# A split-product decoder trunk: all low-part subtractions on VectorE, the norm's squares on ScalarE

## The chip, the cores and the metric

The kernel runs on one core of one Trainium2 chip. The metric is the device time of one execution in microseconds; the median of three runs of the kernel before is 1012.09 us (1011.86 to 1013.77). Names: PE is TensorE (matmul), PEld its weight load, DVE is VectorE, ACT is ScalarE, POOL is GpSimd, SP is the engine that issues the loads of weights.

## What is computed

Two layers of a decoder trunk over N = 288 token columns: a prompt of 256 and 8 groups of 4 sampled tokens. The model width is 1024, kept as X[128, 8, 288]: 8 tiles of 128 features.

```python
for l in range(DEPTH):                       # 2 layers
    h  = rmsnorm(x, g_mix) @ w_in            # mixer: attention, a gated recurrence, a short convolution
    x  = x + concat(a, o_h, o_c) @ w_out
    x  = x + cross_attn(rmsnorm(x, g_xattn)) @ w_xo
    u  = rmsnorm(x, g_ffn) @ w_up            # 1024 -> 2 * 2816
    a, b = split(causal_dwconv3(u))
    x  = x + (silu(a) * b) @ w_down          # 2816 -> 1024
y = rmsnorm(x, g_final)
```

Inputs and outputs are fp32.

## The kernel before

Products of the mixer's input and output projections and of the FFN are "split": an operand v is written as hi + lo, where hi is v rounded to the type fp32r (by ScalarE, a cast) and lo = v - hi (a subtraction, its result fp32r too). A product is then three matmuls of 128x128 weights with 128x288 columns: hi hi, hi lo, lo hi (`split_product`, L1219, L1220, L1221). Both operands need it: the weights, the normalised input (scaled by the gain only; the 1/rms is applied to the product's result), the mixer's results and the FFN's hidden tiles.

One list of steps (`layer_schedule`) sets the order of the work on every engine. Each engine walks the list and does its own part of each step; semaphores tie them. TensorE fills 8 banks of PSUM in turn.

The up stage has 22 tiles per layer (i = 0 to 21). Tile i has two halves (ab = 0, 1), each 8 split products, so 48 matmuls for a tile. In one turn of the loop come, in this order:

- `round` of the weights of tile i + 2 (ScalarE cast of 128x2048, L1116),
- half 0 on TensorE; VectorE evicts it from PSUM times 1/rms (L1885, L1886); GpSimd copies two small pieces of it (L909, L910); ScalarE multiplies by the first tap (L1157),
- `convolve` of tile i - 1: four fused multiply-adds on VectorE (L1894), then a silu on ScalarE (L1162),
- half 1 likewise,
- `pads` of tile i + 1 on GpSimd (two memsets L901, two small copies L902),
- `gate` of tile i - 1: VectorE forms the hidden tile hT (L1903, L1904), ScalarE casts it (L1166), GpSimd subtracts to get hT_lo (L886),
- `rest` of tile i + 2: the weights' lo. VectorE does the first 1024 columns (L1630), GpSimd the other 1024 (L875). TensorE waits for both before tile i + 2.

For w_down a chunk holds 8, 8 or 6 tiles of 256 columns; VectorE does 3 tiles (768 columns) and GpSimd the rest. For w_in and w_out VectorE does all 1024 columns.

```python
LO_DVE = {"in": 8, "out": 8, "up": 4, "down": 3}         # tiles of the weights' lo on VectorE
# GpSimd, step "rest", L870:
pool.wait_ge(w_hi, count)
cols = slice(LO_DVE[args[0]] * width, tiles * width)
pool.drain()
g_.tensor_tensor(lo[:, cols], both[:, cols], hi_part[:, cols].bitcast(F32), ALU.subtract).then_inc(w_lo_pool, 1)
```

The residual adds: after each result tile m of `out`, `xo` and `down` VectorE adds it to X[:, m] (L1555), squares the sum (L1545, L1547) and adds the square to `acc` (L1549). A ones matmul (`ssq`) sums `acc` over the features, and 1/rms is made by ScalarE and four VectorE instructions. ScalarE scales X[:, m] by the next norm's gain into fp32 `XG` (L963) and, after `xo` and `down`, rounded into the hi part (L965, L967); GpSimd subtracts the two to get `xg_lo` (L881, L919), for which TensorE waits in each first split product. At the very end (`down` of the last layer) the same chain leads to the final norm.

Of the kernel before, what the change touches and what calls it, by code (L numbers as in the profile page):

```python
# [28 lines left out]
ALU = mybir.AluOpType  # L29
# [6 lines left out]
P = 128  # L36
# [45 lines left out]
LO_DVE = {"in": 8, "out": 8, "up": 4, "down": 3}  # L82
# [333 lines left out]
def decoder_kernel(nc, a, out):  # L416
# [4 lines left out]
    with ExitStack() as ctx:  # L421
# [39 lines left out]
        def ph(*shape, parts=P):  # L461
# [80 lines left out]
        xg_lo = rounded["XG"]  # L542
        ring_lo = rounded["ring"]
# [33 lines left out]
            "x_square", "sumsq", "xg_tile", "mg_even", "mg_odd", "rms_guess", "sigmoids", "gates_ready", "silu_gate_in",  # L577
# [6 lines left out]
        w_lo_dve = sem("w_lo_dve")  # L584
        w_lo_pool = sem("w_lo_pool")
# [18 lines left out]
        def split_of(kind, i, l):  # L604


            if kind in ("in", "out"):
# [7 lines left out]
                    ring_hi[split % SLOTS], 256, tiles)  # L615

# [115 lines left out]
        def _(pool):  # L732
# [34 lines left out]
            for l, step, args, who in banks.steps:  # L767
# [102 lines left out]
                elif step == "rest" and args[0] in ("up", "down"):  # L870
                    count, both, lo, hi_part, width, tiles = split_of(*args)
                    pool.wait_ge(w_hi, count)
                    cols = slice(LO_DVE[args[0]] * width, tiles * width)
                    pool.drain()
                    g_.tensor_tensor(lo[:, cols], both[:, cols], hi_part[:, cols].bitcast(F32),  # L875
                                     ALU.subtract).then_inc(w_lo_pool, 1)
                elif step == "xo":
                    k = args[0]
                    pool.wait_ge(s["xg_hi"], KT_D * (2 * l + 1) + k + 1)
                    pool.drain()  # L880
                    g_.tensor_tensor(xg_lo[:, k], XG[:, k], xg_hi[k].bitcast(F32), ALU.subtract).then_inc(s["xg_lo"], 1)  # L881
                elif step == "gate":
                    i = args[0]
                    pool.wait_ge(s["h_hi"], FT * l + i + 1)
                    pool.drain()
                    g_.tensor_tensor(hT_lo[:, i], hT[:, i], hT_hi[:, i].bitcast(F32), ALU.subtract).then_inc(s["h_lo"], 1)  # L886
# [25 lines left out]
                elif step == "down" and l + 1 < DEPTH:  # L912
                    k = args[0]
                    if k == 0:
                        pe_done(pool, l, "up", FT - 1, 1)
                        layer_loads(l + 1)
                    pool.wait_ge(s["xg_hi"], KT_D * (2 * l + 2) + k + 1)
                    pool.drain()
                    g_.tensor_tensor(xg_lo[:, k], XG[:, k], xg_hi_mix[:, k].bitcast(F32), ALU.subtract).then_inc(s["xg_lo"], 1)  # L919
# [10 lines left out]
        def _(act):  # L930
# [21 lines left out]
            def gained(l, stage, k):  # L952
# [9 lines left out]
                if stage or l:  # L962
                    ac(XG[:, k], X[:, k], ACT.Identity, scale=par[:, c:c + 1]).then_inc(s["xg_tile"], 1)  # L963
                if stage == 0:
                    ac(xg_hi_mix[:, k], X[:, k], ACT.Identity, scale=par[:, c:c + 1]).then_inc(s["xg_hi"], 1)  # L965
                if stage == 2:
                    ac(xg_hi[k], X[:, k], ACT.Identity, scale=par[:, c:c + 1]).then_inc(s["xg_hi"], 1)  # L967

            for l, step, args, who in banks.emptying_steps:
# [115 lines left out]
                elif (step, args) == ("out", (7,)):  # L1085
                    pe_done(act, l, "hstate_s", 1)
                    for k in range(KT_D):
                        gained(l, 1, k)
# [95 lines left out]
        def _(pe):  # L1184
# [23 lines left out]
            def xg(l, stage, k):  # L1208
                pe.wait_ge(s["xg_tile"], 24 * l + 8 * stage + k + 1 - KT_D)
                return XG[:, k]  # L1210

            def project(out_, w, cols, l, stage):
                for k in range(KT_D):
                    last = mm(out_[:, 0:N], w[:, k, cols], xg(l, stage, k), start=k == 0, stop=k == KT_D - 1)  # L1214
                return last
# [14 lines left out]
            for l, step, args, who in banks.steps:  # L1230
# [209 lines left out]
                elif step == "xq":  # L1440
                    last = project(o, whole(l, P_XQ + args[0]), slice(0, P), l, 1)
# [76 lines left out]
                elif step == "y":  # L1518
# [3 lines left out]
                    pe.wait_ge(s["xg_tile"], 24 * DEPTH - KT_D + 4 * h + 4)  # L1522
# [8 lines left out]
        def _(dve):  # L1531
# [9 lines left out]
            def squares(k, stage):  # L1541

                drain()
                if k == 0:
                    v.tensor_tensor(acc[:], X[:, k], X[:, k], ALU.mult)  # L1545
                else:
                    v.tensor_tensor(sqr[:], X[:, k], X[:, k], ALU.mult)  # L1547
                    drain()
                    last = v.tensor_tensor(acc[:], acc[:], sqr[:], ALU.add)  # L1549
                    if k == KT_D - 1:  # L1550
                        last.then_inc(s["sumsq"], 1)
# [33 lines left out]
            for l, step, args, who in banks.emptying_steps:  # L1585
# [40 lines left out]
                elif step == "rest":  # L1626
                    count, both, lo, hi_part, width, tiles = split_of(*args)
                    dve.wait_ge(w_hi, count)
                    cols = slice(0, LO_DVE[args[0]] * width)
                    v.tensor_tensor(lo[:, cols], both[:, cols], hi_part[:, cols].bitcast(F32),  # L1630
                                    ALU.subtract).then_inc(w_lo_dve, 1)
# [267 lines left out]
                elif step == "gate":  # L1899
# [5 lines left out]
                                    ALU.mult).then_inc(s["h_tile"], 1)  # L1905

# [26 lines left out]
```

## Time and profile before

| what | value |
|---|---|
| median of 3 runs | 1012.09 us (1011.86 to 1013.77) |
| span of the profiled execution | 1012.0 us, 0.1 us under the median |
| PE, PEld | 932.8 us (92%), 869.0 us (86%) busy |
| DVE | 680.2 us (67%) |
| ACT | 435.5 us (43%) |
| POOL | 460.2 us (45%) |

Matmuls are pipelined: the busy time of one (about 0.29 us) overlaps that of the next, which starts 0.13 us after it. So TensorE is best read by the starts of its matmuls and by the idle time before them. The profile gives no time of the profiled execution apart from its span.

### The profile page before, as it was taken

Reading aid. Unit: us, or ns where it says so; the run is one execution under the profiler, and the core shown is the slowest. Engines: PE = TensorE matmul, PEld = TensorE weight load, DVE = VectorE, ACT = ScalarE, POOL = GpSimd, SP = SyncE. Lnnn points to the kernel's source line nnn. Section 1 sums busy time; section 2 is a strip of 40 time slices with the busy share of each in tenths; the row PEclk is TensorE's granted clock in tenths of the full one; section 3 lists DMA queues with packets and bytes.
Section 4 is the critical chain, followed back from the end, with each engine's and each line's share of the span. In section 5 each row is a group of like instructions: output and inputs, shape, how many; then the busy total and the mean of one; then the engine's idle time right before and its main releaser. Section 6 shows DMA issues by size and latency. Waiting matters only on the chain.

```text
span 1012.0 us, 17881 instructions
## 1 busy us (share of the span) xinstructions
PE 932.8 (92%) x6566; PEld 869.0 (86%) x6566; DVE 680.2 (67%) x1260; ACT 435.5 (43%) x728; POOL 460.2 (45%) x701
## 2 busy tenths in 40 slices
PE   6889999998988889889989999999898899898996
PEld 4889988986788888889989998898588888888996
DVE  5567863654459999984455886276345999999533
ACT  4543541434545454444444254143355454453432
POOL 1412310422347777767651231043134777777651
PEclk9989997998689999999999999889868999999999
DMA  8745521566145454445557552139704454453442
GB/s 250 192 114 149 161 72 34 143 183 199 34 118 141 127 159 131 139 143 167 158 147 181 166 166 82 42 98 229 199 1 125 126 163 129 135 158 115 157 146 64
DMA packets 209409, 137.71 MB, mean 136 GB/s; under 512 B 23475, under 2 KB 202203, under 8 KB 209323
## 3 DMA queue, kind: packets, MB, share of 16 engines
q1 hardware_dynamic: 199904, 111.11, 39.2%
q0 software_dynamic: 8288, 22.85, 7.8%
q10 hardware_dynamic: 1131, 2.62, 0.7%
q8 instruction: 53, 0.87, 0.4%
q14 instruction: 33, 0.27, 0.1%
HBM read 131.11 MB, written 5.44 MB: 135 GB/s over the span
## 4 chain that ended last, share of the span: by engine, by line
PE 59%; POOL 16%; ACT 9%; issue 8%; DVE 4%; DMA 1%; POOLq 1%; DVEq 1%; ACTq 0%; SPq 0%
PE banks L1219 12%; PE banks L1220 11%; PE banks L1221 11%; POOL ring_r L875 10%; ACT keysT_r L1116 3%; ACT vals_r L1116 3%; POOL phase L909 3%; PE banks L1397 3%; PE banks L1479 2%; PE banks L1362 2%; PE banks L1319 2%; PE banks L1214 2%; POOL phase L902 1%; PE banks L1447 1%; PE banks L1313 1%
## 5 line engine op out<-in xcount | busy, mean ns | idle before, releaser
L1221 PE MATMUL banks<-mix_r,ring_r 128*128 128x288 f32 x1008 | 302.1, 300 | 0.0
L1894 DVE SCALAR_TENSOR_TENSOR phase<-phase,fpar 128x304 f32<-128x304 f32 x176 | 196.6, 1157 | 4.0 <-issue 0.4
L1221 PEld LDWEIGHTS banks<-mix_r,ring_r 128*128 128x128 f32 x1008 | 195.3, 194 | 0.0
L1219 PE MATMUL banks<-mix_r,ring_r 128*128 128x288 f32 x480 | 151.6, 316 | 9.0 <-issue 6.6
L875 POOL TENSOR_TENSOR ring_r<-ring,keysT_r 128x1024 fp32r<-128x1024 f32 (+2 forms) x36 | 98.9, 2746 | 52.2 <-ACT keysT_r L1116 48.4
L1220 PE MATMUL banks<-XG_r,keysT_r 128*128 128x288 f32 x384 | 115.3, 300 | 0.0
L1219 PEld LDWEIGHTS banks<-mix_r,ring_r 128*128 128x128 f32 x480 | 94.3, 196 | 15.4 <-issue 12.0
L1220 PE MATMUL banks<-XG_r,ring_r 128*128 128x288 f32 x352 | 107.0, 304 | 0.0
L1219 PE MATMUL banks<-mix_r,keysT_r 128*128 128x288 f32 x288 | 89.2, 310 | 18.3 <-POOL ring_r L875 17.0
L1116 ACT CAST ring_r<-ring 128x1024 fp32r<-128x1024 f32 x60 | 62.5, 1046 | 97.9 <-DMA ring<-in_w_in 71.6
L1221 PE MATMUL banks<-phase_r,ring_r 128*128 128x288 f32 x352 | 103.1, 293 | 0.0
L1220 PE MATMUL banks<-XG_r,vals_r 128*128 128x288 f32 x320 | 94.4, 295 | 0.0
L875 POOL TENSOR_TENSOR ring_r<-ring,vals_r 128x1024 fp32r<-128x1024 f32 (+2 forms) x32 | 84.5, 2641 | 12.5 <-ACT vals_r L1116 8.0
L1219 PE MATMUL banks<-mix_r,vals_r 128*128 128x288 f32 x240 | 72.2, 301 | 15.8 <-POOL ring_r L875 15.8
L1630 DVE TENSOR_TENSOR ring_r<-ring,ring_r 128x1024 fp32r<-128x1024 f32 x60 | 74.7, 1247 | 14.5 <-ACT ring_r L1116 14.1
L1162 ACT ACTIVATE phase<-phase 128x304 f32<-128x304 f32 x44 | 20.2, 460 | 136.0 <-DVE phase L1894 136.0
L1116 ACT CAST keysT_r<-ring 128x2048 fp32r<-128x2048 f32 (+1 forms) x36 | 66.8, 1861 | 22.1 <-DMA ring<-in_w_down 22.1
L1219 PEld LDWEIGHTS banks<-mix_r,keysT_r 128*128 128x128 f32 x288 | 55.5, 193 | 23.1 <-issue 21.1
L1630 DVE TENSOR_TENSOR ring_r<-ring,keysT_r 128x1024 fp32r<-128x1024 f32 (+1 forms) x36 | 43.7, 1213 | 47.0 <-ACT keysT_r L1116 47.0
L1220 PEld LDWEIGHTS banks<-XG_r,keysT_r 128*128 128x128 f32 x384 | 74.1, 193 | 0.2
L1220 PEld LDWEIGHTS banks<-XG_r,ring_r 128*128 128x128 f32 x352 | 69.3, 197 | 0.2
L909 POOL COPY phase<-phase 128x2 f32<-128x2 f32 x88 | 31.3, 356 | 83.1 <-DVE phase L1886 82.9
(298 smaller groups left out, 2311.7 us busy)
## 6 DMA issues: line engine op xcount, KB each, us to landing
ring<-in_w_up SPq DMA_DIRECT2D x88, 512.0 KB, 5.1
ring<-in_w_in SPq DMA_DIRECT2D x36, 512.0 KB, 3.9
ring<-in_w_down SPq DMA_DIRECT2D x16, 1024.0 KB, 5.2
ring<-in_w_down SPq DMA_DIRECT2D x8, 768.0 KB, 4.9
rawk<-in_cache_k POOLq DMA_DIRECT2D x32, 128.0 KB, 2.6
vals<-in_cache_v POOLq DMA_DIRECT2D x32, 128.0 KB, 2.4
ring<-in_w_in SPq DMA_DIRECT2D x16, 256.0 KB, 4.0
rawk<-in_cache_mem_k POOLq DMA_DIRECT2D x16, 256.0 KB, 4.7
```

What stands on the lines that cost most here:

```text
L875: g_.tensor_tensor(lo[:, cols], both[:, cols], hi_part[:, cols].bitcast(F32), ALU.subtract).then_inc(w_lo_pool, 1)
L909: g_.tensor_copy(ulast[:, j, g, 0:2], u[:, 256:258])
L1116: nc.scalar.copy(hi_part[:, 0:tiles * width], both[:, 0:tiles * width]).then_inc(w_hi, 1)
L1214: last = mm(out_[:, 0:N], w[:, k, cols], xg(l, stage, k), start=k == 0, stop=k == KT_D - 1)
L1219: mm(out_, hi_w, hi_x, start=start, stop=False)
L1220: mm(out_, hi_w, lo_x, start=False, stop=False)
L1221: return mm(out_, lo_w, hi_x, start=False, stop=stop)
L1319: last = mm(o[:, P * c:P * c + P], mg[:, k, P * t:P * t + P], w[:, k], start=k == 0, stop=k == KT_D - 1)
L1362: last = mm(o[:, 0:256], qs[:, P * b:P * b + P], keysT[:, p, b], start=b == 0, stop=b == 7)
L1397: last = mm(o[0:n, at:at + n // 2], hk[r, p, c], q, start=True, stop=True)
L1630: v.tensor_tensor(lo[:, cols], both[:, cols], hi_part[:, cols].bitcast(F32), ALU.subtract).then_inc(w_lo_dve, 1)
L1894: last = v.scalar_tensor_tensor(out=y[ab][:, 0:304], in0=uab[i % 2][ab][:, w:304 + w], scalar=fpar[:, 3 * l + w, c:c + 1], in1=y[ab][:, 0: ...
```

## The change

All subtractions that make a lo part go to VectorE, and the squares of the residual sum to ScalarE:

- `rest` of w_up and w_down: VectorE subtracts all columns (2048, or 1536 in a short chunk) in one instruction; GpSimd has none. One semaphore, `w_lo`, takes the place of two.
- hT_lo: VectorE subtracts tile i - 1 behind the gate of tile i (the last two behind the last gate).
- xg_lo: VectorE makes X * gain - hi in one fused instruction, one tile behind its residual add, as the prologue of the kernel does already (L1593). ScalarE no longer writes the fp32 `XG` where nothing else reads it (after `xo`, and after `down` except in the last layer).
- ScalarE squares X[:, k] into two buffers in turn; VectorE adds them to the sum, one tile behind its residual add. In `out` the last square stands behind the eight scalings of the next norm.
- GpSimd keeps its small copies, memsets and DMAs.

```diff
-LO_DVE = {"in": 8, "out": 8, "up": 4, "down": 3}
@@ GpSimd
-                elif step == "rest" and args[0] in ("up", "down"):
-                    ...
-                elif step == "xo":
-                    ...
-                elif step == "gate":
-                    i = args[0]
-                    pool.wait_ge(s["h_hi"], FT * l + i + 1)
-                    pool.drain()
-                    g_.tensor_tensor(hT_lo[:, i], hT[:, i], hT_hi[:, i].bitcast(F32), ALU.subtract).then_inc(s["h_lo"], 1)
-                elif step == "down" and l + 1 < DEPTH:
+                elif (step, args) == ("down", (0,)) and l + 1 < DEPTH:
+                    pe_done(pool, l, "up", FT - 1, 1)
+                    layer_loads(l + 1)
@@ ScalarE
-                if stage or l:
+                if stage in (1, 3):
                     ac(XG[:, k], X[:, k], ACT.Identity, scale=par[:, c:c + 1]).then_inc(s["xg_tile"], 1)
...
+            def square(l, step, k):
+                wait_emptied(act, l, step, k)
+                if k >= 2:
+                    act.wait_ge(s["sq_added"], (KT_D - 2) * (3 * l + squared[step] - 1) + max(1, k - 2))
+                ac(sq[k % 2][:], X[:, k], ACT.Square).then_inc(s["x_square"], 1)
...
+                elif step == "out":
+                    if args[0]:
+                        square(l, step, args[0] - 1)
+                    if args[0] == 7:
+                        pe_done(act, l, "hstate_s", 1)
+                        for k in range(KT_D):
+                            gained(l, 1, k)
+                        square(l, step, 7)
                 elif step == "xo":
                     ...
                     gained(l, 2, args[0])
+                    square(l, step, args[0])
                 elif step == "down":
                     ...
+                    square(l, step, args[0])
@@ TensorE
-                pe.wait_ge(w_lo_dve, count)
-                if kind in ("up", "down"):
-                    pe.wait_ge(w_lo_pool, count - SPLIT_PIECES * (l + 1))
+                pe.wait_ge(w_lo, count)
@@ VectorE
+            def summed(l, step, k):
+                if k:
+                    dve.wait_ge(s["x_square"], squares_before(l, step) + k + 1)
+                    drain()
+                    last = v.tensor_tensor(acc[:], sq[0][:] if k == 1 else acc[:], sq[k % 2][:], ALU.add)
+                    last.then_inc(s["sq_added"] if k < KT_D - 1 else s["sumsq"], 1)
+
+            def xg_rest(l, step, k):
+                ...
+                v.scalar_tensor_tensor(out=xg_lo[:, k], in0=X[:, k], scalar=par[:, c:c + 1], in1=hi_part.bitcast(F32),
+                                       op0=ALU.mult, op1=ALU.subtract).then_inc(s["xg_lo"], 1)
...
                 v.tensor_tensor(X[:, m], X[:, m], b_[:, 0:N], ALU.add).then_inc(emptied["D"], 1)
-                squares(m, 0)
+                for k in {0: (), KT_D - 1: (m - 1, m)}.get(m, (m - 1,)):
+                    if step == "xo" or (step == "down" and l + 1 < DEPTH):
+                        xg_rest(l, step, k)
+                    summed(l, step, k)
...
-                    cols = slice(0, LO_DVE[args[0]] * width)
+                    cols = slice(0, tiles * width)
                     v.tensor_tensor(lo[:, cols], both[:, cols], hi_part[:, cols].bitcast(F32),
-                                    ALU.subtract).then_inc(w_lo_dve, 1)
+                                    ALU.subtract).then_inc(w_lo, 1)
...
+                    for t in {0: (), FT - 1: (i - 1, i)}.get(i, (i - 1,)):
+                        dve.wait_ge(s["h_hi"], FT * l + t + 1)
+                        v.tensor_tensor(hT_lo[:, t], hT[:, t], hT_hi[:, t].bitcast(F32), ALU.subtract).then_inc(s["h_lo"], 1)
```

## Rows read from the trace of the kernel before

**Rows 1.** Busy time by stage: us, busy (instructions) of each engine, clock, DMA share, GB/s
```profile
301.20:443.60 142.40, 125.94 (x912) 122.00 (x912) 135.56 (x210) 68.44 (x95) 105.47 (x191) 1.00 0.50 139
```

**Rows 2.** TensorE's timeline: start, us, matmul, [idle before it <- releaser]
```profile
301.21 0.37 PE L1219 MATMUL banks<-mix_r,vals_r 128*128 128x288 f32 x1 [1.10 <-POOL ring_r L875]
...
443.63 0.37 PE L1219 MATMUL banks<-phase_r,vals_r 128*128 128x288 f32 x1 [1.12 <-POOL ring_r L875]
451.13 0.37 PE L1219 MATMUL banks<-phase_r,vals_r 128*128 128x288 f32 x1 [0.92 <-issue]
...
786.47 0.37 PE L1219 MATMUL banks<-mix_r,vals_r 128*128 128x288 f32 x1 [1.12 <-POOL ring_r L875]
...
928.73 0.37 PE L1219 MATMUL banks<-phase_r,vals_r 128*128 128x288 f32 x1 [1.12 <-POOL ring_r L875]
```

**Rows 3.** TensorE's timeline without stalls, the 1st and the 49th of 49 matmuls
```profile
287.29 0.29 PE L1220 MATMUL banks<-XG_r,keysT_r 128*128 128x288 f32 x1
...
293.68 0.29 PE L1220 MATMUL banks<-XG_r,vals_r 128*128 128x288 f32 x1
```

**Rows 4.** VectorE's timeline over one turn of the up loop
```profile
325.08 0.42 DVE L1885 TENSOR_TENSOR phase<-banks,Rn 128x256 f32<-128x256 f32 x1 [0.19 <-issue]
...
325.52 0.42 DVE L1903 TENSOR_TENSOR phase<-phase 128x256 f32<-128x256 f32 x1
...
325.96 1.24 DVE L1630 TENSOR_TENSOR ring_r<-ring,vals_r 128x1024 fp32r<-128x1024 f32 x1
...
327.66 4.71 DVE L1894 SCALAR_TENSOR_TENSOR phase<-phase,fpar 128x304 f32<-128x304 f32 x4
332.56 0.42 DVE L1885 TENSOR_TENSOR phase<-banks,Rn 128x256 f32<-128x256 f32 x1 [0.19 <-issue]
```

**Rows 5.** Inside that turn: the second of the four on VectorE, and GpSimd
```profile
328.66 2.65 DVE L1894 SCALAR_TENSOR_TENSOR phase<-phase,fpar 128x304 f32<-128x304 f32 x1
...
328.56 2.42 POOL L875 TENSOR_TENSOR ring_r<-ring,vals_r 128x1024 fp32r<-128x1024 f32 x1 [0.16 <-issue]
```

**Rows 6.** The layer's first convolve and rest: VectorE, then GpSimd at that time
```profile
292.03 2.04 DVE L1894 SCALAR_TENSOR_TENSOR phase<-phase,fpar 128x304 f32<-128x304 f32 x4 [0.20 <-ACT phase L1157]
294.17 0.42 DVE L1885 TENSOR_TENSOR phase<-banks,Rn 128x256 f32<-128x256 f32 x1
...
296.49 1.22 DVE L1630 TENSOR_TENSOR ring_r<-ring,vals_r 128x1024 fp32r<-128x1024 f32 x1
297.63 0.42 DVE L1885 TENSOR_TENSOR phase<-banks,Rn 128x256 f32<-128x256 f32 x1
...
291.93 0.20 POOL L902 COPY phase<-ust 128x16 f32<-128x16 f32 x1
292.06 0.18 POOL L909 COPY phase<-phase 128x2 f32<-128x2 f32 x1
292.18 0.45 POOL L910 COPY phase<-phase 128x16 f32<-128x16 f32 x1
```

**Rows 7.** From xo to up: VectorE, GpSimd, TensorE, then TensorE's busy time and clock
```profile
269.27 0.45 DVE L1555 TENSOR_TENSOR X<-X,banks 128x288 f32<-128x288 f32 x1
...
276.79 0.46 DVE L1549 TENSOR_TENSOR acc<-acc,sqr 128x288 f32<-128x288 f32 x1
277.17 0.45 DVE L1555 TENSOR_TENSOR X<-X,banks 128x288 f32<-128x288 f32 x1
...
278.77 1.86 POOL L881 TENSOR_TENSOR XG_r<-XG,rawk_r 128x288 fp32r<-128x288 f32 x1 [0.77 <-ACT rawk_r L967]
...
280.69 0.61 PE L1219 MATMUL banks<-rawk_r,keysT_r 128*128 128x288 f32 x1 [1.97 <-POOL XG_r L881]
...
280.00:282.00 2.00, 1.31 (x5) 0.50 0.00 0
```

**Rows 8.** The end: the last sum of squares on VectorE, and ScalarE
```profile
1001.95 0.46 DVE L1549 TENSOR_TENSOR acc<-acc,sqr 128x288 f32<-128x288 f32 x1
...
1001.91 1.28 ACT L995 ACT_TABLE_LOAD   x1
```

More of the change, by code:

```diff
@@ L542, in decoder_kernel @@
         xg_lo = rounded["XG"]
+        sq = [sqr, vv]
         ring_lo = rounded["ring"]
@@ L583, in decoder_kernel @@
         w_hi = sem("w_hi")
-        w_lo_dve = sem("w_lo_dve")
-        w_lo_pool = sem("w_lo_pool")
+        w_lo = sem("w_lo")
         block = ctx.enter_context(nc.Block())
@@ L615, in split_of, with squares_before @@
                     ring_hi[split % SLOTS], 256, tiles)
+        squared = {"out": 1, "xo": 2, "down": 3}
+        def squares_before(l, step):
+            return KT_D * (3 * l + squared[step])
         def fill_no(l, step, *args):
@@ L1084, in _ @@
                     take(l, step, args, hsp.rearrange("p k v -> p (k v)"), bank(l, step)[:, 0:P]).then_inc(emptied["A"], 1)
[L1085 to L1088, printed above, removed]
+                elif step == "out":
[6 more added lines that the diff above has]
+                        square(l, step, 7)
                 elif step == "xo":
@@ L1202, in parts_of, with xg, project @@
                 count, _, lo, hi_part, width, _ = split_of(kind, i, l)
-                pe.wait_ge(w_lo_dve, count)
-                if kind in ("up", "down"):
-                    pe.wait_ge(w_lo_pool, count - SPLIT_PIECES * (l + 1))
+                pe.wait_ge(w_lo, count)
                 return [w.rearrange("p (k c) -> p k c", c=width) for w in (hi_part, lo)]
-            def xg(l, stage, k):
-                pe.wait_ge(s["xg_tile"], 24 * l + 8 * stage + k + 1 - KT_D)
+            def xg(l, k):
+                pe.wait_ge(s["xg_tile"], KT_D * l + k + 1)
                 return XG[:, k]
-            def project(out_, w, cols, l, stage):
+            def project(out_, w, cols, l):
                 for k in range(KT_D):
-                    last = mm(out_[:, 0:N], w[:, k, cols], xg(l, stage, k), start=k == 0, stop=k == KT_D - 1)
+                    last = mm(out_[:, 0:N], w[:, k, cols], xg(l, k), start=k == 0, stop=k == KT_D - 1)
                 return last
@@ L1440, in _ @@
                 elif step == "xq":
-                    last = project(o, whole(l, P_XQ + args[0]), slice(0, P), l, 1)
+                    last = project(o, whole(l, P_XQ + args[0]), slice(0, P), l)
                 elif step == "ys":
@@ L1521, in _ @@
                     cols = slice(P * t, P * t + P) if t < 2 else slice(SEQ, N)
-                    pe.wait_ge(s["xg_tile"], 24 * DEPTH - KT_D + 4 * h + 4)
+                    pe.wait_ge(s["xg_tile"], KT_D * DEPTH + 4 * h + 4)
                     for k in range(4 * h, 4 * h + 4):
@@ L1539, in put @@
                 return bank(l, step, *args)
[L1541 to L1545, printed above, removed]
-                else:
[L1547 to L1551, printed above, removed]
+            def summed(l, step, k):
[5 more added lines that the diff above has]
+            def xg_rest(l, step, k):
+                if step == "xo":
+                    dve.wait_ge(s["xg_hi"], KT_D * (2 * l + 1) + k + 1)
+                    c, hi_part = par_col(R_FFN, l, k), xg_hi[k]
+                else:
+                    dve.wait_ge(s["xg_hi"], KT_D * (2 * l + 2) + k + 1)
+                    c, hi_part = par_col(R_MIX, l + 1, k), xg_hi_mix[:, k]
+                v.scalar_tensor_tensor(out=xg_lo[:, k], in0=X[:, k], scalar=par[:, c:c + 1], in1=hi_part.bitcast(F32),
+                                       op0=ALU.mult, op1=ALU.subtract).then_inc(s["xg_lo"], 1)
             def residual(l, step, m):
```

19 lines of the change are left out of this document (1 added, 18 removed).

## The prediction

> **What bounds the kernel now.** I read the page first, then the chain that ended last, the busy time by stage, and last the timelines of TensorE, VectorE and GpSimd over one turn of the up loop. On the page TensorE looks full and GpSimd half idle. The chain says otherwise for the up stages: there it runs through GpSimd's weight subtraction (L875), ScalarE's cast and GpSimd's copies, tile after tile, not through matmuls. The busy time by stage shows why [rows 1]: over 19 tiles of 142.40 us VectorE is busy for 135.56 us, 95%, GpSimd for 105.47 us.
>
> TensorE's own pace is read where nothing stalls it: 48 matmuls, one tile, from 287.29 to 293.68, 6.39 us [rows 3]; I take 6.40. In the loop a tile takes (443.63 - 301.21) / 19 = 7.50 us in the first layer and (928.73 - 786.47) / 19 = 7.49 us in the second, and the stall ahead of a tile is put down to GpSimd's L875 [rows 2]. So 1.1 us of each tile is not TensorE's.
>
> VectorE's turn takes 332.56 - 325.08 = 7.48 us [rows 4]: eviction of half 0 and the gate, 0.44 us each by starts; the weights' lo and the second eviction, 1.70 together; the four multiply-adds of `convolve`, 4.90 to the next start. The last is the strange one. The same four instructions take 2.04 us (2.14 to the next start) early in the layer, when GpSimd subtracts nothing [rows 6]. In the loop the second of them alone takes 2.65 us: it begins at 328.66, GpSimd's L875 has begun at 328.56 and takes 2.42 us, and the multiply-add ends 0.33 us after it [rows 5]. It stands still while GpSimd runs. The loop is thus a ring: GpSimd's subtraction holds VectorE, VectorE's late eviction holds GpSimd's copies, these stand ahead of GpSimd's next subtraction, and TensorE waits for that.
>
> **The change, part by part.**
>
> *Up loop, VectorE.* Removed: the wait behind GpSimd, 4.90 - 2.14 = 2.76 us. Moved here: the other 1024 columns of the weights' lo. 256 columns take 0.42 us (L1903 [rows 4]) and 1024 take 1.22 [rows 6], 1.04 ns a column, so 1024 more cost 1.07 us; the first 1024 take 1.14 us by starts where GpSimd is quiet [rows 6]; together 2.21. hT_lo, 288 columns: 0.38 us, the step from L1549 to the next instruction, which has that size [rows 7]. The turn becomes 0.44 + 2.14 + 0.44 + 0.44 + 0.38 + 2.21 = 6.05 us, 0.35 less than TensorE's 6.40. TensorE then sets the pace.
>
> Does a new wait come in? The weights' lo for tile i + 2 ends 3.5 us (0.44 + 0.44 + 0.38 + 2.21) after VectorE starts on half 1 of tile i; TensorE needs it 6.40 us after that, 2.9 us of cover. hT_lo waits for a cast of one turn earlier. Behind it on VectorE stands the weights' lo, with that same cover. GpSimd's pads may be held by the long subtraction until its end; ScalarE needs them for half 0 of the next tile, whose eviction also stands behind that subtraction, so nothing is lost.
>
> Bounds of what the trace does not show, GpSimd's six small copies a turn beside a VectorE that hardly pauses: at best they cost VectorE nothing, at worst each holds it for its own 0.20 us [rows 6], 1.2 us a turn. I take nothing: the free `convolve` ran beside L909 and L910, kept its 2.04 us, and it was L910 that stretched to 0.45 [rows 6].
>
> The Trainium skill (SBUF — State Buffer, section "Who interferes with whom") says that a VectorE instruction with two SBUF inputs and a GpSimd instruction that reads SBUF exclude each other, and that the first to start holds the shared ports for its whole length. Rows 5 agree with it for the long subtraction; by the same rule the copies too would hold VectorE, which rows 6 don't show. By the rule's worst case the sum would be that of the first rival below.
>
> From tile 3 to the first down chunk, 19 tiles: 19 x 6.40 = 121.6 us for 142.42 and 142.26 [rows 2]. **Gain 20.8 + 20.7 = 41.5 us.** Upper end this; lower end with 7.25 us a turn, 4.6 a layer.
>
> *Head of up.* After `xo` VectorE goes X add, square, add: 277.17 is the eighth X add, 269.27 the third, 1.58 us a step [rows 7]. Then come two ScalarE passes and GpSimd's last subtraction, 278.77 to 280.63, stretched by VectorE's weights' lo; TensorE starts that product at 280.69 after 1.97 us idle, and its clock is at 0.50, the 1.2 GHz level [rows 7]. After: X add 0.37, fused subtraction 0.53 (2.14 / 4, [rows 6]), add 0.38, about 1.27 us (X add and add at the step of L1549 [rows 7]). The eighth X add comes at 269.27 + 5 x 1.27 = 275.6, its lo part 1.8 us later (subtraction of tile 6, add of square 6, subtraction of tile 7): 277.4 instead of 280.63, 3.2 us. ScalarE makes two passes a tile as before, the second now the square; if they don't keep up, that is rival 2. With the idle time short the clock should stay up: the 24 matmuls of the second half cost at most 24 x 0.133 = 3.2 us extra at half clock; I take 2.2. Tile 3 waited 1.10 us for its weights [rows 2], and will not: 1/rms, first evictions and the weights' lo on VectorE all come forward with the head, and the lo ends about 1.2 us ahead of TensorE. 3.2 + 2.2 + 1.1 = 6.5; the second layer has the same order. **Gain 12.8 us** (6.4 a layer); bounds 0 (the chain as long as before) and 15.
>
> *Start of down.* The first chunk's 48 matmuls take 451.13 - 443.63 = 7.50 us [rows 2] for 6.40. The subtractions for the next chunks move to VectorE. Before the third chunk TensorE has two chunks, 12.8 us; VectorE has in that time 0.44 + 0.44 + 0.38 + 2.21 for the turn, 2.14 for the last `convolve`, 0.44 + 0.76 for the last gate and two hT_lo and at most 2.21 for the weights, 9.0 us, and waits for ScalarE between. **Gain 1.1 a layer, 2.2 us;** bounds 0 and 2.2. Later chunks stall nowhere before, and VectorE has room.
>
> *Squares in `out`.* The last one stands behind eight scalings on ScalarE, and VectorE waits for it. Behind that wait stands only the 1/rms, which waits for the sum over features, and this comes on TensorE behind two products that need all eight scalings; the whole second product is left to hide one square. Cost nothing; without that cover one square, 0.46 us a layer if it is like VectorE's add of that size [rows 8].
>
> *End.* ScalarE scales, then squares, then VectorE adds. Before, the scaling ends at 1001.91, where the table load starts, and the last sum of squares at 1002.41 [rows 8]. Now a square, taken like the add, and the add of 0.46 with two hand-overs come after 1001.91, about 1002.85. **Loss 0.4 us,** all on the path; upper bound 1.7, if the square wants another activation table (1.28 [rows 8]).
>
> *Sum.* 1012.0 (the profiled span, 0.1 under the median) - 41.5 - 12.8 - 2.2 + 0.4 = 955.9; forecast **956 us**, with a range of its own of 951 to 964.
>
> **The rivals.**
>
> 1. *The small copies hold VectorE.* 6.05 + 1.2 = 7.25 us a turn: VectorE is the bound, 19 x 7.25 = 137.8, gain 9.1 in both layers, the rest as above: 1012.0 - 9.1 - 12.8 - 2.2 + 0.4 = **988 us**. It counts from 0.35 us a turn on. For it: the exclusion of rows 5; against it rows 6.
> 2. *The head keeps its length*, because ScalarE or the add of the squares is late, or tables are swapped: 956 + 13 = **969 us**.
> 3. *GpSimd's copies become the ring's slow member*, held by each long VectorE instruction, so that pads or evictions come late and a tile keeps about 7.3 us: **990 us** with the head. Against: the cover above.
> 4. *Slower.* The long multiply-add has another cause than GpSimd's subtraction and stays at 4.90 with the rest. Then a turn is 7.48 - 0.12 + 1.07 + 0.38 = 8.81 us, 19 x 8.81 = 167.4, 25.0 more a layer: 1012.0 + 50.0 - 12.8 + 0.4 = **1050 us**. It decides from 7.8 us a turn on (7.48 + 12.8 / 38), that is from a `convolve` of 3.9. Against it: 2.04 us without the subtraction, and the end at 328.66 + 2.65 = 331.31 so close behind GpSimd's 330.98 [rows 5].
>
> **How the numbers follow.** Forecast 0.72; rival 1 0.13; rival 2 0.06; rival 3 0.04; rival 4 0.04; 0.01 that gains and losses cancel. A measurement tells about 0.2% (2 us) from no change. Faster 0.95, same 0.01, slower 0.04. The range reaches from 951 (a head gain near its bound) to 984: it holds the forecast, rival 2, and that half of rival 1 in which the copies cost less than about 1.1 us a turn, 0.72 + 0.06 + 0.06 = 0.84.
>
> **What would show it.** Starts of tiles on TensorE 6.40 us apart, with no stall in the loop; `convolve` at 2.1 us with no multiply-add over 0.6; VectorE's turn with about 0.3 us of waiting for TensorE; the weights' lo at 2.3 us; GpSimd's copies stretched, not VectorE's work; the first up product's last operand about 8.1 us after the third X add of `xo` and the clock at 1.00 behind it. The prediction is wrong if tiles keep more than 6.6 us, which multiply-adds over 0.6 us (rival 1), TensorE waiting on VectorE's L1630, or evictions waiting on GpSimd (rival 3) would explain.

## The result, and the profile after

The changed kernel takes 958.74 us (median of 4, 958.05 to 959.32) beside 1012.93 us for the kernel before (4 runs, 1011.86 to 1014.60): a ratio of 0.9463, 95% interval 0.9439 to 0.9486. The forecast was 956, its range 951 to 984. The profiled execution has a span of 957.2 us and a time of its own of 958.85, so 1.65 us lie around the span.

The head of the page, and its chain that ended last by engine:

```profile
span 957.2 us, 17553 instructions
PE 915.7 (96%) x6566; PEld 860.2 (90%) x6566; DVE 627.3 (66%) x1280; ACT 446.6 (47%) x752; POOL 283.6 (30%) x565
...
PE 91%; DVE 4%; DMA 2%; ACT 1%; issue 1%; DVEq 1%; ACTq 0%; SPq 0%
```

GpSimd, which had 16% of that chain before, has left it. It lost 176.6 us of busy time, and VectorE, which took its subtractions over, is busy for 52.9 us less than before: so much of what had counted as VectorE's work was waiting inside instructions (the multiply-adds of `convolve` fell from 196.6 to 85.9 us).

The busy time of the up loop from tile 3 to the first down chunk, the stretch that answers to [rows 1]:

```profile
295.30:416.80 121.50, 121.50 (x913) 121.50 (x912) 112.40 (x231) 71.02 (x96) 74.55 (x153) 1.00 0.58 163
```

TensorE has no idle time in it. Its timeline at the two ends of that stretch in both layers, which answers to [rows 2]:

```profile
295.35 0.30 PE L1213 MATMUL banks<-mix_r,vals_r 128*128 128x288 f32 x1
...
416.95 0.29 PE L1213 MATMUL banks<-phase_r,vals_r 128*128 128x288 f32 x1
...
753.48 0.30 PE L1213 MATMUL banks<-mix_r,vals_r 128*128 128x288 f32 x1
...
875.08 0.29 PE L1213 MATMUL banks<-phase_r,vals_r 128*128 128x288 f32 x1
```

19 tiles take 121.60 us in each layer, 6.40 a tile, where [rows 2] gave 142.42 and 142.26. One turn on VectorE, and GpSimd's copies in it, which answer to [rows 4, 5]:

```profile
333.95 0.42 DVE L1889 TENSOR_TENSOR phase<-banks,Rn 128x256 f32<-128x256 f32 x1 [0.47 <-PE banks L1215]
...
334.82 0.48 DVE L1912 TENSOR_TENSOR phase_r<-phase,phase_r 128x288 fp32r<-128x288 f32 x1
335.22 2.28 DVE L1634 TENSOR_TENSOR ring_r<-ring,vals_r 128x2048 fp32r<-128x2048 f32 x1
...
337.85 2.03 DVE L1898 SCALAR_TENSOR_TENSOR phase<-phase,fpar 128x304 f32<-128x304 f32 x4
340.35 0.43 DVE L1889 TENSOR_TENSOR phase<-banks,Rn 128x256 f32<-128x256 f32 x1 [0.47 <-PE banks L1215]
...
335.33 2.23 POOL L890 COPY phase<-ust 128x16 f32<-128x16 f32 x1
337.99 0.43 POOL L897 COPY phase<-phase 128x2 f32<-128x2 f32 x1 [0.44 <-DVE phase L1890]
338.36 0.52 POOL L898 COPY phase<-phase 128x16 f32<-128x16 f32 x1
```

`convolve` is back at 2.03 us for its four multiply-adds, VectorE waits 0.47 us a turn for TensorE (in 13 of the layer's 19 turns; in those ahead of them it is catching up), and it is GpSimd that is held now: a copy of 16 columns that took 0.20 us early in the layer [rows 6] takes 2.23 beside the weights' subtraction (L1634).

Where the 54.8 us between the two spans lie, by starts on TensorE (the first product of `xo`, tile 3 of up, the first down chunk, the next layer's first product):

| stretch | before | after | gain | forecast |
|---|---|---|---|---|
| up loop, tile 3 to first down chunk, both layers | 142.42 + 142.26 | 121.60 + 121.60 | 41.5 | 41.5 |
| head, start of `xo` to tile 3, both layers | 37.76 + 37.23 | 31.03 + 30.30 | 13.7 | 12.8 |
| first layer: first down chunk to the next layer's first product | 71.72 | 70.43 | 1.3 | 1.1 |
| last layer: first down chunk to the end | 83.23 | 82.10 | 1.1 | 1.1 - 0.4 |
| all else: up to `xo` of the first layer; the second layer's first product to its `xo` | 263.45 + 233.89 | 264.32 + 235.80 | -2.8 | 0 |

(The ends of the spans, not rounded, are 1011.96 and 957.18 us.) Most of the last line is scatter: the same kernel's second profile and those of the experiments give 254.5 to 257.6 us from TensorE's first matmul to `xo`, and 232.8 to 236.6 for the second term. But 1.2 us of the second term are the change's. The second layer's fourth input product, before and after:

```profile
529.10:532.38 3.28, 3.28 (x25) 3.28 (x26) 1.40 (x2) 1.05 (x1) 2.11 (x4) 1.00 0.64 194
...
500.83:505.61 4.78, 4.78 (x24) 4.78 (x25) 1.40 (x2) 1.05 (x1) 2.07 (x4) 0.64 0.54 154
```

TensorE was idle for 2.80 us ahead of it in both, but behind that its granted clock is 1.00 (2.4 GHz) before and 0.64 on average after, so part of the stretch is at the 1.2 GHz level, and the product takes 1.50 us more. Of that 0.3 us had been gained in the first input product. In every run with the inputs' low parts on VectorE this product takes 4.65 to 4.80 us, in every run with them on GpSimd 3.26 to 3.28. So the loss comes with the low parts' move; by which way it reaches the clock, no run shows.

### The profile page after: what moved, and what is told of

It is laid out like the page before. It is cut to its first block, busy times and chain, and to the rows that moved or that the text cites. A ratio compares the mean times of both kernels' runs of the same rounds, so it can differ in the third digit from the quotient of the medians.

```text
span 957.2 us, 17553 instructions
## 1 busy us (share of the span) xinstructions
PE 915.7 (96%) x6566; PEld 860.2 (90%) x6566; DVE 627.3 (66%) x1280; ACT 446.6 (47%) x752; POOL 283.6 (30%) x565
## 4 chain that ended last, share of the span: by engine, by line
PE 91%; DVE 4%; DMA 2%; ACT 1%; issue 1%; DVEq 1%; ACTq 0%; SPq 0%
PE banks L1213 22%; PE banks L1215 21%; PE banks L1214 21%; PE banks L1391 3%; PE banks L1473 2%; PE banks L1356 2%; PE banks L1441 2%; PE banks L1313 2%; PE banks L1208 2%; PE banks L1307 1%; PE banks L1369 1%; PE banks L1323 1%; PE banks L1481 1%; PE banks L1422 1%; DMA ring<-in_w_in 1%
## 5 line engine op out<-in xcount | busy, mean ns | idle before, releaser
L1214 PE MATMUL banks<-XG_r,keysT_r 128*128 128x288 f32 x384 | 113.3, 295 | 0.0
L1634 DVE TENSOR_TENSOR ring_r<-ring,keysT_r 128x2048 fp32r<-128x2048 f32 (+1 forms) x36 | 80.1, 2226 | 35.7 <-ACT keysT_r L1112 35.6
L890 POOL COPY phase<-ust 128x16 f32<-128x16 f32 x88 | 101.4, 1166 | 0.1
L1898 DVE SCALAR_TENSOR_TENSOR phase<-phase,fpar 128x304 f32<-128x304 f32 x176 | 85.9, 529 | 3.7 <-ACT phase L1153 0.4
L1213 PE MATMUL banks<-mix_r,keysT_r 128*128 128x288 f32 x288 | 86.1, 299 | 0.0
L1634 DVE TENSOR_TENSOR ring_r<-ring,ring_r 128x1024 fp32r<-128x1024 f32 x60 | 74.7, 1247 | 16.7 <-ACT ring_r L1112 15.9
L1634 DVE TENSOR_TENSOR ring_r<-ring,vals_r 128x2048 fp32r<-128x2048 f32 (+1 forms) x32 | 70.9, 2216 | 20.1 <-ACT vals_r L1112 20.1
L1153 ACT ACTIVATE phase<-phase,fpar 128x304 f32<-128x304 f32 x88 | 48.6, 554 | 71.1 <-DVE phase L1890 71.1
L1112 ACT CAST vals_r<-ring 128x2048 fp32r<-128x2048 f32 (+1 forms) x32 | 59.5, 1858 | 19.3 <-DMA ring<-in_w_down 19.3
```

What stands on the lines that cost most here:

```text
L890: g_.tensor_copy(u[:, 258:306].rearrange("p (b x) -> p b x", x=6)[:, :, 0:2], ust[:, j, g].rearrange("p (b w) -> p b w", w=2)).then_inc(s[ ...
L1112: nc.scalar.copy(hi_part[:, 0:tiles * width], both[:, 0:tiles * width]).then_inc(w_hi, 1)
L1153: ac(yab[i % 2][ab][:, 0:304], uab[i % 2][ab][:, 0:304], ACT.Identity, scale=fpar[:, 3 * l, c:c + 1]).then_inc(s["u_c0"], 1)
L1213: mm(out_, hi_w, hi_x, start=start, stop=False)
L1214: mm(out_, hi_w, lo_x, start=False, stop=False)
L1898: last = v.scalar_tensor_tensor(out=y[ab][:, 0:304], in0=uab[i % 2][ab][:, w:304 + w], scalar=fpar[:, 3 * l + w, c:c + 1], in1=y[ab][:, 0: ...
```

## Experiments

"Head" is measured below from the first product of up to tile 3: 27.5 us before in both layers, 21.17 after, and 6 x 3.20 = 19.2 if nothing stalled.

**The weights alone.** The kernel before, with one part of the change:

```diff
@@ GpSimd, step "rest" of up and down: removed
@@ TensorE, the wait for GpSimd's part of the weights: removed
@@ VectorE, step "rest"
-                    cols = slice(0, LO_DVE[args[0]] * width)
+                    cols = slice(0, tiles * width)
```

> The kernel before, with the weights' low parts of up and down wholly on VectorE and nothing else moved. Theory (GpSimd's 1024-column subtraction holds VectorE, and nothing else does so for long): VectorE's turn is 0.44 + 2.14 + 0.44 + 0.44 + 2.21 = 5.67 us plus at most one hold of about 0.65 us by GpSimd's 288-column subtraction, under TensorE's 6.40; all of the up loop's 41.5 us and the 2.2 at the first down chunk come here, and 1.1 us a layer at tile 3: 1012.9 - 41.5 - 2.2 - 2.2 = 967 us, range 965 to 971. Rival (every small GpSimd instruction holds VectorE for its own length too): 5.67 + 0.65 + 1.2 = 7.5 us a turn, no gain in the loop, about 1008 to 1013 us. Rival (convolve's 4.7 us has another cause): over 1013 us.

Measured: 966.69 us, ratio 0.954 (0.952 to 0.956). That is the 967 expected. The loop takes 121.60 us in both layers, the head 25.70 and 27.00. So all of the loop's gain comes from this part, as expected, and the rivals that keep the loop at its old length fall. hT_lo is still on GpSimd here (L879); VectorE's four multiply-adds and GpSimd in one turn:

```profile
337.20 2.58 DVE L1885 SCALAR_TENSOR_TENSOR phase<-phase,fpar 128x304 f32<-128x304 f32 x4
339.97 0.42 DVE L1876 TENSOR_TENSOR phase<-banks,Rn 128x256 f32<-128x256 f32 x1 [0.19 <-issue]
...
337.24 1.15 POOL L879 TENSOR_TENSOR phase_r<-phase,phase_r 128x288 fp32r<-128x288 f32 x1 [0.16 <-issue]
```

It still holds VectorE, by 2.58 - 2.03 = 0.55 us, and that fits into the turn. To move it was worth nothing here.

**The norm part undone.** The changed kernel with xg_lo on GpSimd again, ScalarE writing fp32 `XG` for it, and the squares on VectorE.

> The changed kernel with the norm part undone: normalised inputs' low parts on GpSimd again (with the third ScalarE pass that it reads), squares on VectorE again; weights and FFN tiles stay moved. Theory (the head of up was shortened by the norm part): 1.58 us a step again in xo and GpSimd's last subtraction ahead of the last product, so 5 to 7 us a layer come back and 0.4 us at the end is won: 958.7 + 10 to 14 - 0.4 = 968 to 972 us. Rival (the head became shorter because GpSimd's queue no longer held the weights' subtraction, not by the norm part): 958 to 962 us.

Measured: 966.12 us, ratio 0.9534 (0.9518 to 0.955); the head takes 25.73 and 25.26 us. 7.4 us come back, under the 10 to 14 expected: of the 27.5 us of a head 1.1 were tile 3's wait for its weights [rows 2], and these stay away, as they do in the run before (26.35 in the mean). So the heads give back 4.6 and 4.1 us, and the end (0.4) and the second layer's input products (1.2) are shorter again. With the run before, this parts the change: some 47 us from the weights (1013.89 to 966.69, the kernel before run beside it) and 7 from the norm part.

**A subtraction that nobody waits for.** The changed kernel with, at the old place of GpSimd's `rest`, for tiles 3 to 21 of up:

```diff
+                elif step == "rest" and args[0] == "up" and args[1] > 2:
+                    pool.wait_ge(w_hi, split_of(*args)[0])
+                    pool.drain()
+                    src, dst = memT[:].rearrange("p k n -> p (k n)")[:, 0:1024], newS[:].rearrange("p k b v -> p (k b v)")[:, 0:1024]
+                    g_.tensor_tensor(dst, src, src, ALU.subtract)
```

> The changed kernel plus, for each up tile from the fourth on, one GpSimd subtraction of 1024 columns between buffers that nothing else uses then; no engine waits for its result. Theory (GpSimd's two-operand subtraction holds VectorE for its own length, whoever needs the result): VectorE's turn is 5.93 + 2.3 less up to 0.9 for evictions = 7.4 to 8.3 us instead of 6.40, 38 times: 997 to 1031 us, one multiply-add or VectorE subtraction a turn at over 2.5 us. Rival (it was the ring of waits that cost the time, TensorE waiting for GpSimd's result and GpSimd for VectorE's): nobody waits now, 957 to 962 us.

Measured: 1005.16 us, ratio 0.9917 (0.99 to 0.9933), inside the 997 to 1031 expected, though no instruction of VectorE is over the 2.5 us that were expected with it. VectorE and GpSimd in one turn:

```profile
341.00 3.59 DVE L1903 SCALAR_TENSOR_TENSOR phase<-phase,fpar 128x304 f32<-128x304 f32 x4
344.78 0.43 DVE L1894 TENSOR_TENSOR phase<-banks,Rn 128x256 f32<-128x256 f32 x1 [0.19 <-issue]
...
348.68 2.09 DVE L1903 SCALAR_TENSOR_TENSOR phase<-phase,fpar 128x304 f32<-128x304 f32 x1
...
340.86 1.89 POOL L879 TENSOR_TENSOR newS<-memT 128x1024 f32<-128x1024 f32 x1 [0.16 <-issue]
```

The next turn's multiply-adds start at 348.68, 7.68 us after 341.00, and the loop takes 144.59 and 144.71 us: 2.2 and 2.5 us more than before the change, with no engine waiting for GpSimd's result. The ring of waits falls as the cause. What costs the time is VectorE standing still: the four multiply-adds take 3.59 us instead of 2.03, all of it in the first of them, 2.09 us. The turn is 5.93 us of work, 1.56 of hold, and the 0.19 that stands ahead of the eviction as issue. That last piece stands in each of the 19 turns of this run's first loop, none of which waits for TensorE, so the changed kernel's turn needs 6.12 us and its slack against 6.40 is 0.28, not the 0.47 of its wait.

**The same place, only writing.** Two memsets of 1024 columns instead:

```diff
-                    g_.tensor_tensor(dst, src, src, ALU.subtract)
+                    for _ in range(2):
+                        pool.drain()
+                        g_.memset(newS[:].rearrange("p k b v -> p (k b v)"), 1.0)
```

> The changed kernel plus, at the place of the idle subtraction, two GpSimd memsets of 1024 columns (by the trace's memset of 1152 columns, 1.06 us, about 1.9 us in all); no engine waits for them. Theory (only reading instructions hold VectorE): multiply-adds stay at 0.5 us and the time at 957 to 961 us. Rival (a busy GpSimd queue, with its pads and copies behind the long instruction, slows the loop): as slow as with the idle subtraction, over 975 us.

Measured: 956.21 us, ratio 0.9439 (0.9423 to 0.9454), no slower than the changed kernel (and just under the 957 to 961 expected); the loop stays at 121.60. GpSimd is occupied for as long as by the subtraction, and VectorE doesn't notice:

```profile
336.39 2.02 DVE L1903 SCALAR_TENSOR_TENSOR phase<-phase,fpar 128x304 f32<-128x304 f32 x4
...
336.23 2.03 POOL L879 MEMSET newS<- 128x1024 f32 x2
```

**One input instead of two**, `g_.tensor_copy(dst, src)` at that place.

> The changed kernel plus, at the place of the idle subtraction, a GpSimd copy of 1024 columns, one input instead of two; no engine waits for it. Theory (any GpSimd instruction that reads and is long holds VectorE for its own length, 0.95 us like the memset of 1024 columns to 1.9 us like the subtraction): the turn is 5.93 + 0.95 to 1.9 = 6.9 to 7.8 us, 38 times more than 6.40: 977 to 1010 us. Rival (two inputs are needed, which is why the small copies did not hold VectorE): multiply-adds stay at 0.5 us, 956 to 961 us.

Measured: 971.64 us, ratio 0.9596 (0.9571 to 0.962); the loop takes 128.71 and 128.80 us, 6.77 a tile.

```profile
340.68 2.72 DVE L1903 SCALAR_TENSOR_TENSOR phase<-phase,fpar 128x304 f32<-128x304 f32 x4
...
340.52 1.04 POOL L879 COPY newS<-memT 128x1024 f32<-128x1024 f32 x1
```

The hold is 2.72 - 2.03 = 0.69 us, the turn 6.12 + 0.69 = 6.81. The time is under the range expected, which took the copy's whole length as hold; the rival falls all the same: reading one input is enough. So it was not their one input that kept the small copies harmless.

**A quarter of the subtraction**, 256 columns.

> The changed kernel plus the idle GpSimd subtraction at 256 columns instead of 1024. Theory (a hold costs only what is over VectorE's 0.47 us of waiting a turn; 1024 columns held it 1.76 us, so 256 hold it about 0.45): VectorE's wait for TensorE falls from 0.47 to under 0.1 us, the tiles stay at 6.40 to 6.45 us, and the time at 957 to 961 us. Rival (the loss goes with the length of the subtraction, a quarter of the 46 us that 1024 columns cost): 968 to 972 us.

Measured: 958.35 us, ratio 0.9457 (0.944 to 0.9474), the loop at 121.60 us.

```profile
340.07 2.31 DVE L1903 SCALAR_TENSOR_TENSOR phase<-phase,fpar 128x304 f32<-128x304 f32 x4
342.57 0.42 DVE L1894 TENSOR_TENSOR phase<-banks,Rn 128x256 f32<-128x256 f32 x1 [0.19 <-issue]
...
339.94 0.61 POOL L879 TENSOR_TENSOR newS<-memT 128x256 f32<-128x256 f32 x1 [0.16 <-issue]
```

VectorE is held for 2.31 - 2.03 = 0.28 us, its wait for TensorE is gone, and the time has not moved. The theory stands with a smaller slack and a smaller hold than it took: the hold just fits into the 0.28 us, and a hold costs only what is over.

In these three runs GpSimd's instruction takes 1.89, 1.04 and 0.61 us and the hold is 1.56, 0.69 and 0.28: 0.33 to 0.35 us less than the instruction in each, where the multiply-add starts 0.13 to 0.16 us after it. (hT_lo, which starts 0.04 us after the multiply-adds in the first run above, takes 1.15 and holds for 0.55: the difference is not the same for every start.) By an estimate from the three a copy of 0.20 us holds nothing. The Trainium skill (SBUF — State Buffer, section "Who interferes with whom") says that a VectorE instruction with two SBUF inputs contends with a GpSimd instruction that reads SBUF, not with one that only writes it; the memsets' 956.21 us and the copy's 971.64 agree.

**The squares back on VectorE**, with xg_lo left there.

```diff
@@ VectorE, residual()
+                squares(m)                        # X*X into sqr, then acc + sqr, as before
...
-                    summed(l, step, k)
@@ ScalarE: the four calls of square() removed
```

> The changed kernel with the squares of the norm back on VectorE, everything else as changed. Theory (in xo VectorE's steps set when the first up product has its operands): a step is X add, square, add and fused subtraction, 0.37 + 0.37 + 0.38 + 0.53 = 1.65 us instead of the 1.35 of the changed kernel, so the eighth low part comes 1.5 to 2.4 us later, 3 to 5 us for both layers, less the 0.45 at the end: 961 to 964 us. Rival (ScalarE's second pass a tile costs as much as VectorE's, the squares' place makes no difference): 957.5 to 960 us.

Measured: 969.53 us, ratio 0.9572 (0.9555 to 0.9589): 10.8 us over the changed kernel, over twice what the theory gave, and far from the rival; the head takes 26.83 us in both layers, and the 0.45 us expected at the end are not won (82.05 us from the first down chunk, 82.10 in the changed kernel). One step of `xo` on VectorE, the waits of TensorE in the first up product, and its busy time and clock behind them:

```profile
276.40 0.44 DVE L1563 TENSOR_TENSOR X<-X,banks 128x288 f32<-128x288 f32 x1
276.94 0.46 DVE L1536 TENSOR_TENSOR sqr<-X 128x288 f32<-128x288 f32 x1
277.47 0.46 DVE L1538 TENSOR_TENSOR acc<-acc,sqr 128x288 f32<-128x288 f32 x1
277.85 0.51 DVE L1558 SCALAR_TENSOR_TENSOR XG_r<-X,par,mix_r 128x288 fp32r<-128x288 f32 x1
278.28 0.45 DVE L1563 TENSOR_TENSOR X<-X,banks 128x288 f32<-128x288 f32 x1
...
278.41 0.40 PE L1208 MATMUL banks<-mix_r,keysT_r 128*128 128x288 f32 x1 [1.21 <-DVE XG_r L1558]
280.29 0.61 PE L1208 MATMUL banks<-mix_r,keysT_r 128*128 128x288 f32 x1 [1.14 <-DVE XG_r L1558]
...
280.00:285.60 5.60, 4.53 (x17) 4.18 (x18) 4.58 (x7) 1.82 (x2) 0.00 (x0) 0.50 0.00 0
```

A step is 1.88 us, not 1.65: square and sum each need the result just ahead of them (the program has a `drain()` there) and start 0.53 to 0.54 us after it, where an independent instruction of that size starts 0.38 us after. TensorE then waits 0.72 to 1.21 us ahead of each of the last four operands, and behind that its granted clock is 0.50, the 1.2 GHz level, for 5.6 us. The direction was right, the size was not.

**The low parts of the inputs alone back on GpSimd**, squares left on ScalarE, which now makes three passes a tile.

```diff
@@ GpSimd, steps xo and down, as in the kernel before
+                    g_.tensor_tensor(xg_lo[:, k], XG[:, k], xg_hi[k].bitcast(F32), ALU.subtract).then_inc(s["xg_lo"], 1)
@@ VectorE, residual()
-                        xg_rest(l, step, k)
```

> The changed kernel with the normalised inputs' low parts alone back on GpSimd (and the third ScalarE pass that they read), the squares staying on ScalarE. Theory (with this the four combinations are measured, and the subtraction's move pays only when VectorE does not square as well): ScalarE makes three passes a tile, about 1.45 us, and GpSimd's last subtraction ends later than VectorE's: 960 to 966 us. Rival (the squares' move alone brings the head's gain): 957 to 960 us.

**The changed kernel again**, beside it on the same chip.

> The changed kernel once more, beside these two on the same chip, as the measure for them: 957 to 960 us. Between the first product of up and tile 3 21.2 us, the layer's mixer between 219 and 223 us.

Measured: 960.68 us, ratio 0.9477 (0.9463 to 0.9491), and 960.66 us, ratio 0.9465 (0.9444 to 0.9485): no difference. By the times alone nothing is decided: both lie at the border of the two ranges, 960, and the second just over the 957 to 960 expected (its mixer, counted from the fourth input product, took 223.2 us for 219 to 223). The heads decide for the rival: the subtraction's move is not what the head's gain comes from. With the two runs above the four combinations are complete:

| head of both layers, us | squares on VectorE | squares on ScalarE |
|---|---|---|
| xg_lo on GpSimd | 25.73, 25.26 | 21.67, 21.47 |
| xg_lo on VectorE | 26.83, 26.83 | 21.17, 21.17 |

Moving the squares wins 3.8 to 5.7 us a layer. Moving xg_lo wins 0.3 to 0.5 where the squares are gone from VectorE, and costs 1.1 to 1.6 where they are not. In the whole time even the first gain is lost again: with xg_lo on GpSimd the heads take 0.8 us more in all and the end 0.34, but the second layer's fourth input product runs at full clock, and the fifth starts 0.9 us earlier. With xg_lo on GpSimd the hold is seen here too: VectorE's add of a square takes 0.85 us beside it, instead of 0.46.

```profile
276.59 0.85 DVE L1552 TENSOR_TENSOR acc<-acc,vv 128x288 f32<-128x288 f32 x1 [0.19 <-ACT vv L969]
...
276.32 0.81 POOL L879 TENSOR_TENSOR XG_r<-XG,mix_r 128x288 fp32r<-128x288 f32 x1 [0.59 <-ACT mix_r L962]
```

**The sums later.** The waits that the trace shows in the head after the change are TensorE's for VectorE's step in `xo`. The sums are not needed until the ssq matmul behind the first two halves of up, so they can stand behind the low parts:

```diff
@@ ScalarE, step xo
-                    square(l, step, args[0])
+                    for k in {0: (0,), 1: (1,), 7: range(2, 8)}.get(args[0], ()):
+                        square(l, step, k)
@@ VectorE, residual()
-                    summed(l, step, k)
+                    if step != "xo":
+                        summed(l, step, k)
+                if step == "xo" and m == KT_D - 1:
+                    for k in range(KT_D):
+                        summed(l, step, k)
```

> The changed kernel with VectorE's adds of the squares in xo put behind the last low part (and ScalarE's squares from the third on behind its last rounding). Theory (xo's step on VectorE, 1.35 us, is what TensorE waits for at the first up product, 0.46 and 0.32 us ahead of its last two operands): a step falls to X add and subtraction, 0.9 us, the low parts keep ahead of the product, and 1.0 to 1.9 us a layer are won: 955 to 957 us. Rival (the sum of the squares is then what is late, TensorE or the first eviction waiting for it): 958 to 962 us.

Measured: 955.60 us, ratio 0.9419 (0.9398 to 0.9441). A step of `xo` is 0.98 us, and the first up product runs without a wait, at full clock:

```profile
272.12 0.46 DVE L1557 TENSOR_TENSOR X<-X,banks 128x288 f32<-128x288 f32 x1
272.50 0.51 DVE L1552 SCALAR_TENSOR_TENSOR XG_r<-X,par,mix_r 128x288 fp32r<-128x288 f32 x1
273.10 0.45 DVE L1557 TENSOR_TENSOR X<-X,banks 128x288 f32<-128x288 f32 x1
...
273.60:280.20 6.60, 6.60 (x50) 6.52 (x49) 5.15 (x12) 4.31 (x9) 0.47 (x4) 1.00 0.58 159
```

The head falls from 21.17 to 20.08 us in both layers, 1.1 a layer. That shows the gain; the time alone does not, since the changed kernel with the idle memsets took 956.21.

**And the square first at the end.** The same, with `square` ahead of `gained` in the last layer's `down`.

> The kernel with the late sums in xo, and with ScalarE's square ahead of its scaling in the last layer's down. Theory: the late sums win about 1.1 us a layer between the first up product and tile 3 as in the run before it, and at the end the last add of the squares starts 0.5 us after the square instead of behind scaling and square, 1.0 us instead of 1.46 after the X add starts: 955 to 957 us, 2 to 3 us under the changed kernel run beside it. Rival (the scaling, now last, is waited for instead): no gain at the end, as the late sums alone.

Measured: 957.38 us (956.94 to 958.18), ratio 0.9441 (0.9429 to 0.9454), beside 960.66 (957.36 to 962.15) for the changed kernel on the same chip: 0.4 over the range expected, and 3.3 under the kernel beside it instead of 2 to 3. It has the lowest median there; the intervals of the two ratios just overlap, so the times alone don't settle 3 us. The trace shows what is gained: heads of 20.08 us, 1.1 a layer, and at the end the last add starts at 945.30, 1.09 us after its X add at 944.21 and no longer 1.46; the last Newton step ahead of the output comes 947.97 - 944.21 = 3.76 us after the X add instead of 949.85 - 945.72 = 4.13. That is 2 x 1.1 + 0.37 = 2.6 us, less 0.07 a layer by which the up loop is longer (121.66 and 121.67 us); the rest of the 3.3 is not the edits' by anything that the trace shows.

## Why the prediction was right

*Up loop.* Right to the tenth: 41.5 us. VectorE's turn came out at 6.12 us (5.93 of work and the 0.19 ahead of the eviction) against 6.05, with the weights' lo at 2.28; its 0.28 us of slack answer to the 0.35 of the prediction. The cause that it rested on, GpSimd's subtraction holding VectorE, is shown by the idle subtraction; that the ring of waits was only what passed the hold on follows from the same run, and the memsets show that a busy GpSimd alone does not do it. hT_lo's move, 0.38 us in the sum of the turn, was neither needed nor harmful: the loop takes 121.60 us with and without it.

*Small copies, rival 1.* Taken as nothing, and nothing it was: all 78 multiply-adds of the first layer's loop take 0.5 us. The prediction had the rows for it, but not the reason: the copies read, as the copy of 1024 columns does, and that one held VectorE. The rows show that the copies are the ones that are stretched, 0.20 to 2.23 us; that they are too short to hold is the estimate above, and no run varied them.

*Head.* 13.7 us against 12.8, and the closeness is in part luck. (The three terms add up to 6.5 a layer; the prediction carried 6.4.) By starts, the third X add to the last operand was to shorten by 3.2 us, and shortened by 2.8 in each layer (11.42 to 8.65 in the first). From there to tile 3 it was to be 2.2 for the clock and 1.1 for the weights, 3.3, and was 3.55 and 3.1. So the terms came to 12.3. The other 1.4 us lie ahead of the third X add, where the prediction has no term and the same kernel scatters: 5.42 and 4.69 us from the start of `xo`, 5.15 and 5.84 when it ran again, 5.82 and 5.67 before. The head's gain of that second run is 12.8.

The first term was too large because the step of `xo` is 1.35 us, not 1.27: the fused subtraction to the next start takes 0.61 and not 0.53.

```profile
269.74 0.46 DVE L1556 TENSOR_TENSOR X<-X,banks 128x288 f32<-128x288 f32 x1 [0.32 <-PE banks L1481]
...
276.48 0.45 DVE L1556 TENSOR_TENSOR X<-X,banks 128x288 f32<-128x288 f32 x1
276.84 0.51 DVE L1551 SCALAR_TENSOR_TENSOR XG_r<-X,par,rawk_r 128x288 fp32r<-128x288 f32 x1
277.45 0.46 DVE L1540 TENSOR_TENSOR acc<-acc,sqr 128x288 f32<-128x288 f32 x1
277.82 0.51 DVE L1551 SCALAR_TENSOR_TENSOR XG_r<-X,par,rawk_r 128x288 fp32r<-128x288 f32 x1
...
278.39 0.40 PE L1213 MATMUL banks<-rawk_r,keysT_r 128*128 128x288 f32 x1 [0.32 <-DVE XG_r L1551]
...
280.00:282.00 2.00, 2.00 (x17) 2.00 (x17) 1.09 (x1) 0.00 (x0) 0.00 (x0) 1.00 0.00 0
```

The product of the last operand starts 8.65 us after the third X add (269.74), not 8.1. The half clock is gone wholly, 1.00 where [rows 7] had 0.50. The parts were not kept apart either: it is the squares' move that shortens the head; the fused subtraction, which the prediction costed beside it, gives 0.3 to 0.5 us a layer with the squares gone, and without that it costs.

*Start of down.* 1.3 us in the first layer and 1.5 in the second (83.23 to 81.72, read in the run with the weights alone, where the end is unchanged), against 1.1 each. The prediction read the first layer's 7.50 us for both. In the second the first chunk took 7.05 us, but the second chunk, where no stall was expected, took 6.91; after the change each takes 6.29.

*End.* Loss of 0.38 us (82.10 against 81.72), 0.4 forecast; no second table load. The last add starts 1.46 us after its X add, where it was 1.08 (from 1000.87 to the 1001.95 of [rows 8]):

```profile
1000.87 0.46 DVE L1555 TENSOR_TENSOR X<-X,banks 128x288 f32<-128x288 f32 x1 [0.83 <-PE banks L1221]
...
945.72 0.46 DVE L1556 TENSOR_TENSOR X<-X,banks 128x288 f32<-128x288 f32 x1 [1.36 <-PE banks L1215]
...
947.18 0.46 DVE L1540 TENSOR_TENSOR acc<-acc,vv 128x288 f32<-128x288 f32 x1 [0.46 <-ACT vv L957]
...
946.65 0.43 ACT L957 ACTIVATE vv<-X 128x288 f32<-128x288 f32 x1
947.09 1.28 ACT L985 ACT_TABLE_LOAD   x1
```

*Sum.* 958.74 us against 956. The steps gained 57.6 us where 56.1 were forecast. The difference to the other side is what the sum left out: 2.8 us in the stages that it took as unchanged, 1.2 of them the lower clock that comes with the low parts on VectorE, which has no term in the prediction, and the 1.65 us around the span. The kernel before has these too (a later run of it took 1012.69 us, its span 1011.0), so the sum, which started from a span, was one of spans. The mechanism of the loop was right; that the total came within 2.7 us is in part a matter of errors that cancel.

## What to carry to other kernels

When an instruction takes longer in one stage than in another, look at what GpSimd reads at that moment: VectorE won more by taking GpSimd's work over than the work cost it. Such a hold costs only what exceeds the slack of the held engine, so a loop has a length of instruction up to which it is free (here a hold of 0.28 us), and beyond which nearly all of it shows: 1.21 us a tile for the 1.28 over with the idle subtraction, 0.37 for 0.41 with the copy. On a chain of short instructions count from start to start, and count a dependent one higher (0.53 us) than an independent one (0.38, both at 288 columns).

## What the runs showed of the hardware that was not expected

- A GpSimd instruction needs only one SBUF input to hold VectorE's two-input multiply-adds: the copy of 1024 columns, 1.04 us, held them for 0.69. Two memsets of 2.03 us held them for nothing.
- The hold goes both ways: GpSimd's copy of 16 columns, 0.20 us alone, took 2.23 us behind VectorE's subtraction of 2048 columns, in 38 of its 44 turns.
- The same idle time of TensorE, 2.80 us ahead of the second layer's fourth input product, was followed by a granted clock of 1.00 in the kernel before and of 0.64 in the changed one. Why is open.
